# Moving the activations' high and low buffers 64 bytes along each SBUF partition

## The reference

```python
def first_block(x, ...):
    x = x + 0.5 * swiglu(rmsnorm(x, norm_ffn1_g), ffn1_w_gu, ffn1_w_down)   # D_FF = 2816
    x = x + hybrid_mixer(rmsnorm(x, norm_mix_g), w_in, conv_w, ...)          # short conv + gated linear attention
    x = x + 0.5 * swiglu(rmsnorm(x, norm_ffn2_g), ffn2_w_gu, ffn2_w_down)
    return rmsnorm(x, final_norm_g)

def second_block(x, ...):
    proj = rms_norm(x, norm_mix) @ w_in      # neighbourhood attention and retention
    x = x + mix @ w_out
    x = x + jnp.square(jax.nn.relu(rms_norm(x, norm_mlp) @ w_up)) @ w_down   # d_ff = 4096
    return rms_norm(x, norm_final)
```

## Time and profile before

| | |
|---|---|
| median of 3 runs | 1753.23 us (1753.15 to 1754.0) |
| span of the profiled execution, first to last instruction | 1751.3 us |
| TensorE busy | 1744.0 us, 10407 products |
| TensorE weight loads busy (beside the products) | 1534.4 us |
| VectorE busy | 1238.9 us |
| ScalarE busy | 850.4 us |
| DMA | 176.61 MB, 101 GB/s |

### The profile page before, as it was taken

How to read it: one execution, slowest core, us unless ns; L and a number is a source line. 1 busy time by engine, 2 the same in 40 slices (tenths; PEclk the granted TensorE clock), 3 DMA queues, 4 the chain that set the end, 5 groups by cost and what they waited for, 6 DMA issues and landing times.

```text
span 1751.3 us, 26596 instructions
## 1 busy us (share of the span) xinstructions
PE 1744.0 (100%) x10407; PEld 1534.4 (88%) x10407; DVE 1238.9 (71%) x1955; ACT 850.4 (49%) x1442; POOL 38.8 (2%) x38
## 2 busy tenths in 40 slices
PE   9999999999999999999999999999999999999998
PEld 7889989878888899988888998988877888989897
DVE  7949849666776557965795894976688677748474
ACT  6425526454333335743553562654655543627274
POOL 0000000000000000000000000000232000000000
PEclk9999999999999999999999999999999999999999
DMA  5232423332123232333323233334511233333232
GB/s 185 82 109 97 127 89 104 110 110 85 51 86 106 86 108 97 109 111 98 96 88 117 93 110 96 109 109 131 141 61 61 85 96 97 97 96 118 89 120 72
DMA packets 68427, 176.61 MB, mean 101 GB/s; under 512 B 8112, under 2 KB 9392, under 8 KB 68304
## 3 DMA queue, kind: packets, MB, share of 16 engines
q1 hardware_dynamic: 66576, 171.60, 31.4%
q10 hardware_dynamic: 1280, 2.08, 0.3%
q0 software_dynamic: 448, 1.24, 0.3%
HBM read 170.70 MB, written 2.10 MB: 99 GB/s over the span
## 4 chain that ended last, share of the span: by engine, by line
PE 95%; DVE 3%; ACT 1%; issue 1%; DMA 0%; DVEq 0%; ACTq 0%; POOLq 0%
PE ps L2064 18%; PE ps L2066 18%; PE ps L2065 18%; PE ps L2156 10%; PE ps L2158 10%; PE ps L2157 10%; PE ps L2086 2%; PE ps L2087 2%; PE ps L2088 2%; DVE wl L1159 1%; PE ps L2305 0%; ACT BThi L579 0%; PE ps L2435 0%; DVE BTlo L1231 0%; PE ps L2460 0%
## 5 line engine op out<-in xcount | busy, mean ns | idle before, releaser
L2064 PE MATMUL ps<-Ahi,wh 128*128 128x512 f32 x913 | 357.2, 391 | 0.0
L2065 PE MATMUL ps<-Alo,wh 128*128 128x512 f32 x913 | 355.4, 389 | 0.0
L2066 PE MATMUL ps<-Ahi,wl 128*128 128x512 f32 x913 | 355.4, 389 | 0.0
L2156 PE MATMUL ps<-BThi,wh 128*128 128x256 f32 x1232 | 340.6, 276 | 0.3 <-ACT tm L569 0.3
L2157 PE MATMUL ps<-BTlo,wh 128*128 128x256 f32 x1232 | 340.3, 276 | 0.0
L2158 PE MATMUL ps<-BThi,wl 128*128 128x256 f32 x1232 | 340.2, 276 | 0.0
L543 ACT ACTIVATE wh<-raw 128x1024 fp32r<-128x1024 f32 (+1 forms) x206 | 213.1, 1036 | 221.6 <-PE ps L2066 187.4
L1159 DVE TENSOR_TENSOR wl<-raw,wh 128x1024 fp32r<-128x1024 f32 (+1 forms) x206 | 250.1, 1215 | 64.6 <-ACT wh L543 62.6
L2156 PEld LDWEIGHTS ps<-BThi,wh 128*128 128x128 f32 x1232 | 231.3, 188 | 0.6 <-issue 0.6
L2157 PEld LDWEIGHTS ps<-BTlo,wh 128*128 128x128 f32 x1232 | 231.3, 188 | 0.0
L2158 PEld LDWEIGHTS ps<-BThi,wl 128*128 128x128 f32 x1232 | 231.3, 188 | 0.0
(11 more groups left out here) (355 smaller groups left out, 2707.7 us busy)
## 6 DMA issues: line engine op xcount, KB each, us to landing
raw<-in_w_gu SPq DMA_DIRECT2D x128, 256.0 KB, 2.8
raw<-in_w_d SPq DMA_DIRECT2D x32, 512.0 KB, 3.5
raw<-in_w_dn SPq DMA_DIRECT2D x32, 512.0 KB, 3.8
raw<-in_w_up SPq DMA_DIRECT2D x48, 256.0 KB, 2.8
raw<-in_w_gu SPq DMA_DIRECT2D x22, 512.0 KB, 3.6
raw<-in_w_d SPq DMA_DIRECT2D x16, 384.0 KB, 3.1
raw<-in_w_v SPq DMA_DIRECT2D x8, 512.0 KB, 3.8
raw<-in_w_cc SPq DMA_DIRECT2D x8, 512.0 KB, 3.6
```

The source lines that it names most:

```text
L2064: pe.matmul(ps, wh[:, c], hi[:, k, :], start=(k == 0), stop=False)
L2065: pe.matmul(ps, wh[:, c], lo[:, k, :], start=False, stop=False)
L2066: last = pe.matmul(ps, wl[:, c], hi[:, k, :], start=False, stop=(k == nb - 1))
L2156: pe.matmul(ps, whi[:, w], bhi, start=(new and kp == 0), stop=False, skip_group_check=not new)
```

## The change

Two small buffers move ahead: `rt` (64 bytes) now stands between `X` and `Hhi`, `vec` (448 bytes) between `Alo` and `raw`. So `Hhi`, `Hlo`, `Ahi` and `Alo` start 64 bytes later, at 192 modulo 512, and so do the buffers of the second block that are placed inside `Ahi` and `Alo` (`NV`, `ROPE`, `GD`, `RS2`, `RS3`, `YH` and others). `raw`, `wh`, `wl`, `R`, `SS`, `SS2` and the `tm` buffers start 512 bytes later, and keep their places modulo 512. `gfm`, `ident`, `ones` and `st` start 64 bytes later; `rt2`, `small` and the shared region stay where they were. No instruction is added, removed or moved.

```diff
     X, _ = sb("X", [P, KT, T])
+    rt, _ = sb("rt", [P, 16])
     Hhi, oHhi = sb("Hhi", [P, KT, T], F32R)
     Hlo, oHlo = sb("Hlo", [P, KT, T], F32R)
     Ahi, oAhi = sb("Ahi", [P, KT, T], F32R)
     Alo, oAlo = sb("Alo", [P, KT, T], F32R)
+    vec, _ = sb("vec", [P, NVEC])
     RAWS, _ = sb("raw", [P, NRAW, 1024])
...
     TM = [sb(f"tm{i}", [P, T + 2])[0] for i in range(NTMP)]
-    vec, _ = sb("vec", [P, NVEC])
     gfm, _ = sb("gfm", [P, 8])
...
     st, _ = sb("st", [P, 8, 16])
-    rt, _ = sb("rt", [P, 16])
     rt2, _ = sb("rt2", [P, 16])
```

## The result

| | before | after |
|---|---|---|
| median, us | 1753.2 (1753.15 to 1754.0) | 1768.74 (1767.98 to 1770.29) |
| span of the profiled execution, us | 1751.3 | 1766.3 |
| TensorE busy, us | 1744.0 | 1759.9 |

The medians are of four executions each. The ratio is 1.0088, with an interval of 1.0074 to 1.0102. The forecast was 1749.6 us and its range ended at 1754.2, so both the size and the direction were wrong.

What follows compares the result with a forecast made beforehand. TensorE was taken as the bound, busy 1744.0 of 1751.3 us. Terms -2.88 - 0.45 - 0.28 - 0.05 = -3.66, taken as -3.6 us, led from 1753.23 to 1749.6 us; range 1748.8 to 1754.2, at 0.80.

Steps and rivals of the forecast that it cites:

- Units of 512 columns: 0: 4221 products of 512 columns: a load late by up to 0.1 us is hidden by the stream, so no change.
- rival 3: At +64 the stream yields, so 512-column units pay: 4221 x 6.4 ns = +27 us, some 1777 us; chance 0.08.
- What is late is the weight load: 256-column products at distance 0: load and stream disturb one another, and the load comes out 6 to 7 ns later.
- I take 0.1133 us, since -64 is the nearest distance shown, 64 bytes off as well: 256-column products on `A` and `H`, moved to +64, were taken to cost 0.1133 us, as at -64.
- mixer's pairs: 12 pairs of 84 products of 256 columns, each going from 9.76 to 9.52 us: -2.88 us.
- the split blocks: Nine units ending in 6 products of 256 columns at distance 0, gaining 0.05 us each: -0.45 us.
- the last unit: Its first 30 products go from 3.59 to 3.40 us, the other 18 save another 0.1: -0.28 us together.
- `wide` steps: 0: 128 columns of `H` load while `wh` moves, at distance -64 after the change; 512-column products, so no cost.
- `BThi` pairs unchanged: Pairs of 84 products of 256 columns on `BThi`, distance still -64, were to stay at 9.52 us.
- the distance is not what matters: Rival: 256-column products of `A` and `H` stay at 0.120 us, time 1753.2 us; chance 0.23, part gains included.
- The terms for ScalarE and VectorE: Any effect on their accesses lies within a 15 ns spread and beside TensorE: 0; busy times within 2 us.
- the cover: Between 700 and 760 us VectorE, making the mixer's weights, would go from 90% to 93% and still keep up.

Runs made afterwards that it cites:

- the grid: Products and weight loads alone, no other engine beside TensorE, 8 moving places by 8 weights' places; 512 columns took 226.7 to 233.3 ns, 256 columns 113.3 to 120.0.

## Why the prediction was wrong, step by step

**The step that failed is "Units of 512 columns: 0".** It rested on this picture: at a bad distance the *load* comes late, and 512 columns leave it 0.114 us to hide in. The runs show that the product comes late although no load does: at +64 three products in a row take 6.7 ns more in the cheap regime (228.9 each on average) and 20 ns more in the dear one (233.3 each), while the load beside each lasts its 188 ns and is over some 40 ns ahead of the next product. 4221 unit products and the first 48 cost 11.6 us, or 2.7 ns each. This is rival 3 in its mechanism, sized at 6.4 ns a product and +27 us. That is near the size of the dear regime, which held for some 210 of 1400 groups of three products. I gave it 0.08, on the strength of the earlier trace rows. Those rows were too weak to carry the term: one product each, printed to 0.01 us, against an effect of 2 ns; and the load beside it was for a float32 product. At this resolution ten products or more in a row are needed to see 2 ns. By their printing, the rows allow a product to be anywhere from 220 to 240 ns, so the bound that they give for 4221 products reaches from below nothing to 4221 x 13.3 ns = +56 us, all of it inside a term that I set to 0. The other half of the picture, "What is late is the weight load", is shown only in part. The loads before read 189 ns under the 256-column products on `Ahi` and 188 to 189 on `MThi`, while the products differ by 6.7 ns; in the grid they last 192 ns at distance 0 and 188 to 189 at the others. Which of the two waits for the other is not settled for 256 columns.

**"I take 0.1133 us, since -64 is the nearest distance shown, 64 bytes off as well"** failed next. Distance has a sign: 256 columns cost 117.8 ns at +64, and at -64 113.3 in the cheap regime. The mixer's pairs gave 12 x 0.05 = 0.6 us in place of 2.9, the split blocks and the last unit 0.13 us together in place of 0.73.

**"`wide` steps: 0"** was the same mistake as with the units. Distance -64, 233 ns in place of 227, 384 products, +2.2 us. The prediction noticed that their distance changes and dismissed it by the width.

**`BThi` pairs unchanged** held for 36 of 44. The others fell into the dear regime; the 44 together cost +1.8 us. That an untouched operand can pay because of what ran ahead of it was in none of my rivals.

**What held.** 120 against 113 ns in the earlier trace rows was read correctly as an effect of the distance, and 1753.2 us by "the distance is not what matters" was rightly doubted. The Trainium skill, "TensorE: Matmul & The Clock Gate", in "Step-by-step: what each phase is for", says that loading the next weights takes no read bandwidth from the running matmul. The traces don't agree: with nothing else at work, moving the stream by 64 bytes against the loaded weights changes a 512-column product from 226.7 to 228.8 ns. A reader who took the rule as it stands would have forecast 1753.2 us. The terms for ScalarE and VectorE were right (+0.5 and +1.0 us, beside TensorE), and so was the cover. The busy times between 700 and 760 us after, which answer to the earlier trace rows:

```profile
700.00:760.00 60.00, 60.00 (x522) 60.00 (x521) 56.49 (x102) 46.35 (x94) 0.00 (x0) 1.00 0.34 109
```

VectorE is at 94% and TensorE still never idle.

**What stays open.** Why two regimes exist, and which beginnings lead into which. Why distance 0 costs 3 to 7 ns at other widths and nothing at 512 columns. No run streams products without a load beside each; that the load is the partner follows from the grid, where the cost goes by the distance between the two and not by the place of either. Nothing here shows the inside of the memory; "distance modulo 256" is a description that fits the kernels here, not a mechanism. A layout with `A` at 0 for units and at -64 for the mixer's pairs would need second copies of the weights at shifted places; by 12 x 0.24 us it would bring 2.9 us at best. It wasn't tried. No kernel here beats the one before.

## What to carry to other kernels

When TensorE streams without a gap, lay out the moving operand and the weights that are loaded beside it together: for places in steps of 64 bytes what counts is their distance modulo 256, and the best one depends on the width (0 for 512 columns, -64 for 256 as long as the cheap regime holds), so a move that helps one shape has to be weighed against the count of the others. Here 102 + 432 products could gain and 4653 could lose. Measure a cost of 1% over a long row of equal products, from start to start, and never take a zero from two rows of the timeline.

## What the runs showed of the hardware

- Moving operand and loaded weights, at places in steps of 64 bytes, interact by their distance modulo 256: 226.7, 228.9, 232.1 to 233.3 and 233.3 ns for 512 columns at 0, 64, 128 and 192; 120.0, 117.8, 118.6 to 118.8 and 113.3 or 117.8 ns for 256 columns.
- Under 512 columns the loads last 188 ns at every distance and end 36 to 43 ns ahead of the next product: the product comes late without a late load.
- At 0, 64 and -64 the means fit sums of one size, 6.7 ns, none, one, two or three of them in three products: 226.7, 228.9 and 233.3; 113.3, 117.8 and 120.0. That is 16 periods of 2.4 GHz. The single starts don't show such a step: at +64 the three distances read 226, 229 and 232 ns. The values at 128 lie between.
- At +64 with 512 columns and at -64 with 256 there are two regimes. A sequence stays in one for up to 110 us, three products in a row issued as halves switched it, and the same instructions ran in either in two executions.
- With both operands 16 bytes past a multiple of 32 a 512-column product costs 233.3 ns even at distance 0, in the one case tried.
- Even at the best distance a 512-column product takes 0.443 ns a column, where a column per period would be 0.417.
